# Additive masks of the prompt attention as bfloat16 products in a streaming-encoder step

## The reference

```python
def _fox_attention(q, k, v, cq, ck, qpos, kpos):          # 8 heads of 64
    s = einsum('bqhd,bkhd->bhqk', q, k) * scale
    s = s + cq[..., :, None] - ck[:, :, None, :]           # sums of the log forget gates
    mask = kpos[None, :] <= qpos[:, None]                  # causal
    p = softmax(where(mask, s, -inf), axis=-1)
    return einsum('bhqk,bkhd->bqhd', p, v)

def _diff_attention(q, k, v, lam, qpos, kpos):             # 4 heads, 2 components of 64
    s = einsum('bqhcd,bkhcd->bhcqk', q, k) * scale
    mask = (kpos[None, :] // 64) <= (qpos[:, None] // 64)  # causal in blocks of 64
    p = softmax(where(mask, s, -inf), axis=-1)
    a = p[:, :, 0] - lam * p[:, :, 1]
    return einsum('bhqk,bkhe->bqhe', a, v)
```

## Time and profile before

| what | value |
|---|---|
| timed runs | 1579.19, 1606.29 and 1615.05 us |
| their median | 1606.29 us |
| profiled execution, first to last instruction (its span) | 1580.9 us |
| mean granted clock of TensorE in it, as a share of full speed | 0.880 |
| TensorE busy | 1262.5 us, 80% of the span |
| VectorE, ScalarE busy | 457.0 us, 308.7 us |

### The profile page before, as it was taken

One profiled execution on the slowest core, in us unless ns is written; L12 is line 12 of the kernel. 1 busy time (PEld: TensorE's weight loads), 2 busy tenths in 40 slices (PEclk: granted clock), 3 DMA queues, 4 the chain that ended last, 5 costly groups with the idle time before them and its releaser, 6 DMA issues. The chain is left out here.

```text
span 1580.9 us, 17362 instructions
## 1 busy us (share of the span) xinstructions
PE 1262.5 (80%) x6567; PEld 797.1 (50%) x6568; DVE 457.0 (29%) x1072; ACT 308.7 (20%) x671; POOL 87.3 (6%) x119
## 2 busy tenths in 40 slices
PE   5997998599798688999887923889787778777760
PEld 4876666377666476789756821333222222222220
DVE  5331233152345444451534252111100010100105
ACT  7111232240133434231333210000000000000001
POOL 1013000000000000000000003000000000000003
PEclk9996599699999699999997955999888998899995
DMA  7127500212600502433163161976999999999986
GB/s 239 67 95 273 221 1 8 64 54 102 225 11 9 180 30 83 157 133 144 70 223 128 40 225 28 338 273 222 398 396 398 398 395 395 395 396 398 397 316 226
DMA packets 147518, 322.11 MB, mean 204 GB/s; under 512 B 22401, under 2 KB 24337, under 8 KB 147457
## 3 DMA queue, kind: packets, MB, share of 16 engines
q1 hardware_dynamic: 137536, 296.04, 50.6%
q0 software_dynamic: 7328, 15.81, 2.9%
q10 hardware_dynamic: 2592, 9.44, 1.5%
HBM read 291.25 MB, written 32.55 MB: 205 GB/s over the span
## 5 line engine op out<-in xcount | busy, mean ns | idle before, releaser
L1903 PE MATMUL bank<-ring,xT 128*64 128x512 f32 x1152 | 299.7, 681 | 95.9 <-DMA ring<-in_w 94.6
L1903 PEld LDWEIGHTS bank<-ring,xT 128*64 128x64 f32 x1152 | 93.7, 157 | 300.4 <-issue 180.4
L1923 PE MATMUL bank<-ring,hT 128*64 128x512 f32 x576 | 127.6, 594 | 18.0 <-ACT hT L1954 13.0
L1989 DVE TENSOR_TENSOR hh<-bank,sg 128x512 f32<-128x512 f32 x18 | 12.4, 691 | 373.4 <-PE bank L1903 373.4
L241 PE MATMUL bank<-ident 128*128 128x128 f32 x216 | 39.6, 360 | 72.8 <-PEq L1649 33.8
L1923 PEld LDWEIGHTS bank<-ring,hT 128*64 128x64 f32 x576 | 47.5, 137 | 86.5 <-issue 86.5
L202 DVE TENSOR_TENSOR ring_r<-ring,ring_r 128x512 fp32r<-128x512 f32 x128 | 80.8, 696 | 6.6 <-ACT ring_r L197 6.4
L225 PE MATMUL bank<-ring_r,nT_r 128*128 128x512 f32 x200 | 79.6, 398 | 0.0
L1950 ACT ACTIVATE sg<-bank 128x512 f32<-128x512 f32 x18 | 10.8, 597 | 332.8 <-PE bank L1903 332.8
L241 PEld LDWEIGHTS bank<-ident 128*128 128x128 f32 x216 | 37.2, 269 | 75.8 <-issue 75.8
L197 ACT CAST ring_r<-ring 128x512 fp32r<-128x512 f32 x128 | 69.0, 616 | 13.7 <-PEq L1510 13.7
(11 more groups left out here) (398 smaller groups left out, 2060.3 us busy)
## 6 DMA issues: line engine op xcount, KB each, us to landing
ring<-in_w SPq DMA_DIRECT2D x96, 2048.0 KB, 19.7
ring<-in_w_in SPq DMA_DIRECT2D x6, 2048.0 KB, 13.0
expert_rows<-fpzero SPq DMA_DIRECT2D x20, 512.0 KB, 14.2
expert_rows<-yb ACTq DMA_DIRECT2D x18, 512.0 KB, 6.2
ring<-in_cache_mem_k SPq DMA_DIRECT2D x8, 1024.0 KB, 6.7
ring<-in_cache_mem_v SPq DMA_DIRECT2D x8, 1024.0 KB, 9.2
ring<-in_cache_fox_k SPq DMA_DIRECT2D x8, 512.0 KB, 4.9
ring<-in_cache_fox_v SPq DMA_DIRECT2D x8, 512.0 KB, 5.7
```

What stands on the lines that cost most here:

```text
L1903: ins = nc.tensor.matmul(ps[2 + m][64 * x:64 * x + 64, :], xT[:, k, 64 * x:64 * x + 64], w(2 * m + x)[:, k, :], start=k == 0, stop=k == KT ...
L1923: ins = nc.tensor.matmul(ps[5 + half][64 * x:64 * x + 64, :], hT[:, k, 64 * x:64 * x + 64], w(4 + x)[:, k, half * 512:(half + 1) * 512], s ...
L1989: nc.vector.tensor_tensor(hh[:, :], ps[3][:, :], sg[:, :], ALU.mult).then_inc(hid_done, 1)
```

## The change

The identity and the mask get bfloat16 copies, and the mask product reads those. 0, 1 and -1e30 are held in them (-1e30 rounded to bfloat16). The copies are made by VectorE at the start of each of the two stages: first the identity's, which is in SBUF already, then, when its DMA has landed, the mask's. TensorE waits behind its warm-up for both copies, in place of the DMA. The order of the products on TensorE is the same, and so are the turns, the warm-up and everything else that reads the float32 identity. The memory attention has no mask and is as before.

```diff
             with ExitStack() as c:
                 mask = None if mem else sb(c, tag + "mask", [P, P])
+                mask_b = None if mem else sb(c, tag + "maskb", [P, P], BF16)
+                ident_b = None if mem else sb(c, tag + "identb", [P, P], BF16)
+                narrowed = None if mem else sem(c, tag + "narrowed")
...
-                                nc.tensor.matmul(b[:, n - P:n], ident[:, :], mask[:, :], start=True, stop=False,
+                                nc.tensor.matmul(b[:, n - P:n], ident_b[:, :], mask_b[:, :], start=True, stop=False,
                                                  skip_group_check=True)
...
                             warm_up(ps[0])
-                            pe.wait_ge(md, 16)
+                            pe.wait_ge(narrowed, 2)
...
+                        if not mem:
+                            nc.vector.tensor_copy(ident_b[:, :], ident[:, :]).then_inc(narrowed, 1)
+                            dve.wait_ge(md, 16)
+                            nc.vector.tensor_copy(mask_b[:, :], mask[:, :]).then_inc(narrowed, 1)
                         todo = []
                         for u, (qt, h, cc) in enumerate(units):
```

## The result

| | runs, us | median |
|---|---|---|
| before, in the same job | 1579.19, 1606.29, 1612.24, 1615.05 | 1609.26 |
| changed | 1608.32, 1613.68, 1618.43, 1623.73 | 1616.06 |

The ratio is 1.0241, 95% interval 1.0153 to 1.033; it leaves out runs of a kernel that lie more than 1.5% above its shortest, which here sets the changed kernel against 1579.19 alone, so I also give all runs: by the medians the change costs 6.8 us, by the means of four 12.8. Its profiled execution took 1618.43 us, with a span of 1616.5.

The account below looks back on a forecast made before the run. TensorE was taken to set the pace in both stages. Mask products at -13 us and the diff stage's clock at +8 gave -5, set against the median of 1606.3: 1601 us, range 1574 to 1626 us.

Parts of the forecast that it names:

- The copies and the new wait: Start of each stage, two VectorE copies and TensorE's wait for them: cost nothing, hidden by the warm-up.
- The mask products: 32 in each stage: shorter slots save 8.5 us in the fox stage and 4.4 in the diff stage, together 13 us.
- The clock in the diff stage: Diff stage: clock falls to half soon after 424 us and comes back in tile 1, costing 8 us.
- The clock in the fox stage: Fox stage: half clock from 144.0 us and the rise at 205.4 us stay as profiled, no term in the sum.
- the rival that I gave 0.12: Fox stage, out-turns of tile 1: the rise at 205.4 us goes missing, +28 us, 1629 us in all; chance 0.12.
- Rival 3: Fox stage: clock rises a tile earlier, about 168 us, 17 us less; sum -30, 1576 us; chance 0.12.
- rival 2: Fox stage stays at half clock after 205.4 us: -13 + 8 + 28 = +23, 1629 us; chance 0.12.

## Why the prediction was wrong, step by step

Two steps of the sum failed: the copies and their wait, set at nothing, and the clock of the fox stage, left as it was in the one profile. The second is the larger, 33 us at the float32 price against 8, and the kernel stays slower when the wait is taken away. The forecast went 5 us down and the kernel went up; that 1616 us lies inside the range is luck, as the range was wide for the spread of the runs.

- **The copies and the new wait: a step that failed.** I set them at nothing, with VectorE idle and 0.31 us for a copy. VectorE was idle, but GpSimd was not: its addition, which needs 11 us from 137 us on, stands in the same block, and the prediction left it out. The copy waited for its end, and TensorE with it: 7.9 to 8.4 us, shown by three runs (gone with ScalarE, gone with the addition held back, there with float32 products). The Trainium skill has this in "SBUF — State Buffer", section "Who interferes with whom": VectorE's `copy` and `cast` can, in modes that use two ports, take a port pair that GpSimd shares; whoever issues first keeps it for the whole instruction, and the other waits. The traces agree: 10.29 us beside the addition, 0.23 without it, 0.30 on ScalarE.
- **The mask products: right, a little too small.** I took 0.17 us a slot at full clock and 0.34 at half. The traces show savings of 0.16 and 0.25 in the diff stage at full clock and 0.42 at half clock. With the whole fox stage at half clock that is 13.5 us there.
- **The clock in the diff stage: right in kind, too small in size.** It stayed at half clock for 29 us, 8 us past tile 1's first long turn at 471.1, up to which I had priced it. The stage grew by 5.8 us while its slots, by the forecast, saved 4.4, so the clock cost about 10, where I took 8.
- **The clock in the fox stage: the larger step that failed, and the rival that I gave 0.12.** The sum kept the rise at 205.4 us and with it 14 of the 32 units at full clock. In the changed kernel's profile the clock never came back, and all 32 were at half. Had the mask products been as before, this would have cost 135.0 - 101.9 = 33 us against the profile of before; I priced the rival at 28. Behind it stands a mistake of method: I set the sum against the median while reading the clock from one execution. The kernel before has two outcomes about equally often, and the profile was the lucky one. Of the changed kernel's runs, and of the two with the wait removed, none of 12 is of the lower kind, against 19 of 37 of before: as far as 12 runs can show, the change took that outcome away. The rival took the place for decided by the mask product behind the out-turns; but with the addition behind the copies the clock rose at 252.2 us behind turns and values alone, so a mask product at that place isn't needed for a rise.

The account closes on the other outcome, whose 18 runs have a median of 1612.5 us. Its fox stage is at full clock for the first 4 us and takes 132.4 us, so the changed one, 121.5, saves 10.9 there. Less 10.9, plus 5.8 in the diff stage, plus 7.9 of wait is 1615, against a measured median of 1616.06; without the wait 1607, against 1604.63 and 1608.42.

Two readings in the prediction are put right here. Rival 3's sum leaves out the 8 us of the diff stage, which rival 2 counts; with them it is 1584 us. And the rise at 205.4 us did not come right behind seven transposes: there are three turns, then value products, four out-turns and a mask product in front of it, so it doesn't speak against the sentence on transposes that rival 2 names.

The rival that the clock is chance alone fails: all 22 runs with more mask products in the fox stage (six or eight in bfloat16, in one kernel eight and then four, or two in float32) lie between 1548.75 and 1572.52 us, and the diff stage is at half clock from its first tile in all four profiles with one bfloat16 product a unit there (changed, copies on ScalarE, addition behind the copies, diff stage alone) and in no other. What stays open: what decides, in the kernel before, whether a given execution gets its rise at the end of tile 1, and whether work over fewer rows would have held the clock.

## What to carry to other kernels

Before adding an instruction to an idle engine, look at what the other engines do at that moment, GpSimd beside VectorE first; here the copy that feeds TensorE was safe on ScalarE (0.30 us beside the addition). Where TensorE is the bound, a cheap product may be the one that keeps the clock up: here making it cheaper cost more than it saved, and repeating it paid. And where the runs of a kernel spread over more than the change is worth, a single profile shows one of their outcomes; count with all of them.

## What the runs showed of the hardware that I had not expected

- TensorE can be busy without a gap for 121.5 us and stay at 1.2 GHz, and with more products over 128 rows between its 64-row and 4-row ones do the same stage in 76.8 us at 2.4 GHz, though it has more to do.
- A VectorE copy of 128 x 128 elements took 10.29 us beside a 10.97 us GpSimd addition, and 0.99 us beside a 0.95 us GpSimd memset, which reads nothing; with GpSimd quiet it took 0.23 us.
- A chain of eight bfloat16 products of 128 columns with their weight loads takes 0.54 us at full clock (150.61 to 151.15 in the run with eight), the change from the rows of the product before included:

```profile
150.61 0.61 PE L796 MATMUL bank<-fpmaskb,fpidentb 128*128 128x128 bf16 x8
151.15 0.70 PE L798 MATMUL bank<-fkT,fqT 64*128 64x256 f32 x2
```
